# Attention's way back to channel layout: eight TensorE transposes against one VectorE transpose and a DMA round trip, with the conv branch placed first

## The reference

```python
h = rmsnorm(x, norm_mix_g[l])
proj = h @ w_in[l]
q, k, v, c_b, c_c, c_u, g_attn, g_conv = jnp.split(proj, split_idx, axis=-1)
...
attn = diff_attention(q1, q2, k1, k2, vh, rel_bias, lam)
attn = rmsnorm(attn, subln_g[l], SUBLN_EPS) * (1.0 - lambda_init)
y_attn = attn.reshape(B, T, ATTN_W) @ w_branch_attn[l]
y_conv = (c_b * causal_depthwise_conv(c_c * c_u, conv_w[l])) @ w_branch_conv[l]
merged = jax.nn.sigmoid(g_attn) * y_attn + jax.nn.sigmoid(g_conv) * y_conv
x = x + merged @ w_out[l]
```

## Time and profile before

| | |
|---|---|
| median of 3 runs | 1074.43 us (1073.64 to 1075.0) |
| profiled execution | 1073.29 us, span 1071.3 us |
| PE busy | 1063.6 us, 99% of the span |
| DVE, ACT, POOL busy | 746.9, 596.5, 185.1 us (70%, 56%, 17%) |
| granted TensorE clock | 0.999 of full speed |

### The profile page before, as it was taken

The page is one execution under the profiler, slowest core; times in us unless marked ns, Lnnn a source line. Parts: engine busy times, 40 slices in busy tenths (PEclk is TensorE's granted clock), DMA queues, the critical chain, the costliest instruction groups (busy, mean ns, idle before and its releaser), DMA issues.

```text
span 1071.3 us, 16564 instructions
## 1 busy us (share of the span) xinstructions
PE 1063.6 (99%) x5396; PEld 903.4 (84%) x5396; DVE 746.9 (70%) x948; ACT 596.5 (56%) x861; POOL 185.1 (17%) x337
## 2 busy tenths in 40 slices
PE   9999999999999999999999999999999999999997
PEld 7888888888889888888888888888888998888886
DVE  6766657868687866665776666668787888666654
ACT  7555445555785754444555444445657756555463
POOL 0354320000340022220002223000003300222300
PEclk9999999999999999999999999999999999999999
DMA  7888786655786688776668877566457957888872
GB/s 248 257 258 243 244 265 202 200 169 162 216 275 198 210 246 244 238 238 193 190 211 251 243 243 223 181 217 188 150 165 246 301 176 218 253 241 261 259 242 79
DMA packets 204551, 236.82 MB, mean 221 GB/s; under 512 B 17780, under 2 KB 179360, under 8 KB 204368
## 3 DMA queue, kind: packets, MB, share of 16 engines
q1 hardware_dynamic: 189968, 198.82, 59.6%
q0 software_dynamic: 14128, 36.76, 11.6%
q10 hardware_dynamic: 400, 0.51, 0.1%
HBM read 217.41 MB, written 18.62 MB: 220 GB/s over the span
## 4 chain that ended last, share of the span: by engine, by line
PE 98%; DVE 1%; DMA 0%; ACT 0%; issue 0%; DVEq 0%; ACTq 0%
PE acc L1636 21%; PE acc L1617 17%; PE acc L1618 17%; PE acc L1619 17%; PE acc L1645 11%; PE acc L1715 2%; PE acc L1714 2%; PE acc L1712 2%; PE acc L1640 1%; PE acc L1835 1%; PE mixed L1640 1%; PE score L1640 1%; PE acc L1836 1%; PE acc L1837 1%; PE score L1855 0%; DVE w_lo L1064 0%
## 5 line engine op out<-in xcount | busy, mean ns | idle before, releaser
L1064 DVE TENSOR_TENSOR w_lo<-raw,w_hi 128x1024 fp32r<-128x1024 f32 x382 | 455.6, 1205 | 226.5 <-ACT w_hi L657 225.7
L657 ACT CAST w_hi<-raw 128x1024 fp32r<-128x1024 f32 (+1 forms) x381 | 390.7, 1037 | 313.3 <-PE acc L1619 206.0
L1617 PE MATMUL acc<-w_hi,xm 128*128 128x512 f32 x816 | 319.6, 392 | 0.0
L1619 PE MATMUL acc<-w_lo,xm 128*128 128x512 f32 x816 | 318.0, 390 | 0.0
L1618 PE MATMUL acc<-w_hi,xm 128*128 128x512 f32 x816 | 317.9, 390 | 0.0
L1636 PE MATMUL acc<-hm,w_hi 128*128 128x512 f32 x656 | 206.3, 396 | 0.0
L1619 PEld LDWEIGHTS acc<-w_lo,xm 128*128 128x128 f32 x816 | 153.2, 188 | 31.8
L1617 PEld LDWEIGHTS acc<-w_hi,xm 128*128 128x128 f32 x816 | 153.3, 188 | 31.6
L1618 PEld LDWEIGHTS acc<-w_hi,xm 128*128 128x128 f32 x816 | 153.3, 188 | 31.2
L1645 PEld LDWEIGHTS acc<-hm,w_lo 128*128 128x128 f32 x720 | 133.4, 188 | 28.9
L532 POOL DMA_DIRECT2D hid_scratch<-sum x176 | 96.3, 554 | 346.5 <-DVE sum L1166 344.8
(11 more groups left out here) (191 smaller groups left out, 881.2 us busy)
## 6 DMA issues: line engine op xcount, KB each, us to landing
raw<-in_ffn_w_gate_dram SPq DMA_DIRECT2D x176, 256.0 KB, 3.1
raw<-in_ffn_w_up_dram SPq DMA_DIRECT2D x176, 256.0 KB, 3.6
raw<-in_ffn_w_down_dram SPq DMA_DIRECT2D x164, 256.0 KB, 3.5
raw<-in_w_in_dram SPq DMA_DIRECT2D x160, 256.0 KB, 3.3
hid_scratch<-sum POOLq DMA_DIRECT2D x176, 64.0 KB, 3.1
part<-hid_scratch POOLq DMA_DIRECT2D x44, 256.0 KB, 3.4
raw<-in_w_out_dram SPq DMA_DIRECT2D x32, 256.0 KB, 3.3
gate_scratch<-acc_lo POOLq DMA_DIRECT2D x64, 64.0 KB, 3.1
```

What stands on the lines that cost most here:

```text
L657: nc.scalar.copy(w_hi[:, s, 0:tiles, :], raw[:, s, 0:tiles, :]).then_inc(hi_split, 1)
L1064: nc.vector.tensor_tensor(w_lo[:, s, 0:tiles, :], raw[:, s, 0:tiles, :], w_hi[:, s, 0:tiles, :], ALU.subtract).then_inc(lo_split, 1)
L1617: nc.tensor.matmul(s[:, t, :], xh, wh[:, k], start=not u and not k, stop=False, skip_group_check=True)
L1619: mm = nc.tensor.matmul(s[:, t, :], xh, wl[:, k], start=False, stop=(u, k) == (GU_UNITS - 1, GK - 1), skip_group_check=True)
```

## The change

The eight PE transposes and the semaphore wait in front of them go. DVE turns the scaled attention in 32 x 32 blocks (into `v_tok`, which is free by then), POOL writes these to DRAM with four DMAs of 128 KB and reads them back with one of 512 KB (into `part`), and ACT applies the gain from there. POOL does this between the second and the third gate set. The order of the branches is exchanged: conv gates are projected as the first two sets, the conv branch is made ready first and multiplied first. Unrelated to this, in the first feed-forward block `join_squares()` moves ahead of one `lo()`.

```diff
-            gates[:, KT:KT + 4, :], gates[:, KT + 4:2 * KT, :], proj[:, 0:4, :], proj[:, 4:8, :])]
+            gates[:, 0:4, :], gates[:, 4:KT, :], proj[:, 0:4, :], proj[:, 4:8, :])]
+        attn_blocks_at = v_tok.rearrange("p t n -> p (t n)")
+        attn_back_at = part.rearrange("p k n -> p (k n)")
...
+        def gate_tile(n):
+
+            return (KT + 4 * n) % (2 * KT)
...
-                    by_token(w_in, l, GATE_COL + g * HALF)
+                    by_token(w_in, l, GATE_COL + gate_tile(g) * P)
...
-                    for w in (w_branch_attn, w_branch_conv):
+                    for w in (w_branch_conv, w_branch_attn):
...
-            def shuffle_gates():
+            def shuffle_attn(layer):
+
+                pool.wait_ge(attn_blocks, layer)
+                for a in range(QUARTERS):
+                    pool.dma_start(attn_dram.rearrange("(b i) (a f) -> a i b f", b=QUARTERS, a=QUARTERS)[a],
+                                   attn_blocks_at[a * QUARTER:(a + 1) * QUARTER, :].rearrange(
+                                       "i (b f) -> i b f", b=QUARTERS)).then_inc(attn_out, 16)
+                pool.wait_ge(attn_out, 16 * QUARTERS * layer)
+                pool.dma_start(attn_back_at, attn_dram).then_inc(attn_back, 16)
+
+            def shuffle_gates(layer):
 
                 for g in range(GATE_SETS):
+                    if g == 2:
+                        shuffle_attn(layer)
...
                 hi()
-                wait(act, (attn_turned, layers.now))
-                for b in range(2):
-                    last = nc.scalar.activation(
-                        attn[:, 2 * b:2 * b + 2].rearrange("p h t d -> p (h t d)"), side[b], ACT.Copy,
-                        scale=cur[:, P_SUBLN:P_SUBLN + 1])
-                last.then_inc(attn_gained, 1)
-                hi()
+                hi()
+                wait(act, (conv_ready, layers.now))
+                nc.scalar.copy(mix[:, N_HEADS:, 0:SEQ], conv).then_inc(conv_hi, 1)
+                hi()
+                wait(act, (attn_back, 16 * layers.now))
+                nc.scalar.activation(attn[:, :, :, :].rearrange("p h t (a n) -> p (h t) a n", a=QUARTERS),
+                                     attn_back_at.rearrange("p (a m n) -> p m a n", a=QUARTERS, m=N_HEADS * QT),
+                                     ACT.Copy, scale=cur[:, P_SUBLN:P_SUBLN + 1]).then_inc(attn_gained, 1)
                 wait(act, (attn_gained, layers.now))
                 nc.scalar.copy(mix[:, 0:N_HEADS, 0:SEQ],
                                attn[:, :, :, :].rearrange("p h t d -> p h (t d)")).then_inc(attn_hi, 1)
                 hi()
-                hi()
-                wait(act, (conv_ready, layers.now))
-                nc.scalar.copy(mix[:, N_HEADS:, 0:SEQ], conv).then_inc(conv_hi, 1)
                 have_table(ACT.Sigmoid)
                 gate_of_set()
...
                 for p in range(1, XPAIRS):
                     add_square(p)
+                join_squares()
                 lo()
-                join_squares()
                 lo()
...
                 taps(0)
                 lo()
+                wait(dve, (attn_scaled, layers.now))
+                nc.vector.transpose(attn_blocks_at.rearrange("p (b m n) -> p b m n", b=QUARTERS, m=N_HEADS * QT),
+                                    attn[:, :, :, :].rearrange("p h t (b n) -> p b (h t) n", b=QUARTERS)
+                                    ).then_inc(attn_blocks, 1)
                 taps(1)
...
-                wait(pe, (attn_scaled, layers.now))
-                for h in range(N_HEADS):
-                    for t in range(QT):
-                        col = ((h % 2) * QT + t) * P
-                        mm = nc.tensor.transpose(side[h // 2][:, col:col + P], attn[:, h, t, :], ident[:, :])
-                mm.then_inc(attn_turned, 1)
                 others_by_token()
...
-                            multiply(new_set(merge_sets[2 * n + j], len(merge_sets)), [mix[:, n * UK + k, :] for k in range(UK)], True, True,
+                            multiply(new_set(merge_sets[2 * n + j], len(merge_sets)), [mix[:, (1 - n) * UK + k, :] for k in range(UK)], True, True,
```

More of the change, by code:

```diff
@@ L225, in trunk @@
         gate_raw = [v.rearrange("p k n -> p (k n)") for v in (
-            gates[:, KT:KT + 4, :], gates[:, KT + 4:2 * KT, :], proj[:, 0:4, :], proj[:, 4:8, :])]
+            gates[:, 0:4, :], gates[:, 4:KT, :], proj[:, 0:4, :], proj[:, 4:8, :])]
+        attn_dram = nc.dram_tensor("attn_scratch", (P, N_HEADS * SEQ), F32, kind="Internal").ap()
         gate_dram = [nc.dram_tensor(f"gate_scratch{g}", (P, 2 * PAIR * SEQ), F32, kind="Internal").ap()
@@ L301, in trunk @@
         gate_by_token, gate_turned, gate_out = sem("gate_by_token"), sem("gate_turned"), sem("gate_out")
+        attn_blocks, attn_out, attn_back = sem("attn_blocks"), sem("attn_out"), sem("attn_back")
         gate_back = [sem(f"gate_back{g}") for g in range(GATE_SETS)]
@@ L610, in _ @@
             pool.wait_ge(bias_loaded, 32)
-            shuffle_gates()
+            shuffle_gates(1)
             shuffles()
             shuffles()
-            shuffle_gates()
+            shuffle_gates(2)
             pool.wait_ge(conv_ready, DEPTH)
@@ L1009, in _ @@
                         for j in range(2):
-                            t = n * 2 * PAIR + j * PAIR
+                            t = gate_tile(n) + j * PAIR
                             last = nc.scalar.activation(
@@ L1496, in _ @@
                 lo()
+                wait(dve, (conv_hi, layers.now))
+                nc.vector.tensor_tensor(mix[:, N_HEADS:, SEQ:2 * SEQ], conv, mix[:, N_HEADS:, 0:SEQ],
+                                        ALU.subtract).then_inc(mix_lo, 1)
+                lo()
                 wait(dve, (attn_hi, layers.now))
@@ L1501, in _ @@
                 lo()
[L1502 to L1505, removed]
                 turn_gates()
@@ L1515, in _ @@
                             n = 2 * g + j
-                            g_at = gates[:, bass.ds(i * (2 * PAIR) + (g * KT + j * PAIR), PAIR), :]
+                            g_at = gates[:, bass.ds(i * (2 * PAIR) + ((1 - g) * KT + j * PAIR), PAIR), :]
                             p_at = part[:, j * PAIR:(j + 1) * PAIR, :]
```

## The result

The changed kernel takes 1079.61 us (median of four runs, 1078.97 to 1083.93) against 1074.47 for the kernel before (1073.64 to 1075.0). The ratio is 1.0061 with an interval of 1.0049 to 1.0073: slower by 0.6%. The forecast was 1075.4, its range ended at 1079.0. The profiled execution took 1078.97 us with a span of 1077.1, that is 5.8 us more than the earlier trace rows were read from (1071.3).

A forecast was written before the change was run, and what follows sets the result against it. PE bounds the kernel and any lateness is paid in full. Waits of 2 x 1.5 less 1.74 and 0.23 gained give +1.0 us: 1074.3 against the profiled execution, 1075.4 on the timed runs' scale; range 1072.3 to 1079.0.

The forecast's parts named there:

- forecast 1.97: Gain on PE: eight transposes gone, 1.74 us over two layers, plus 0.23 us at the start from the moved `join_squares()`.
- T: Landing of the attention's read back from DRAM, first layer: forecast 312.4, bounds 310.3 and 313.5.
- b4: Branch-loop unit after b3: its `w_lo` ready at T + 8.5, wanted by PE at 319.4, 1.5 us late per layer.
- s: PE's wait at b4 in each layer, T - 310.9: 1.5 us at T = 312.4.
- b3: First attention unit of the branch loop: ready at T + 4.8, wanted at 316.5, late only from T = 311.7 on.
- b1: Branch-loop unit needing the conv product: DVE subtracts until 309.1, PE wants it at 310.8; expected to stay covered.
- I take 3.7: POOL's wait for the attention's four 128 KB writes to land, in us; 64 KB writes showed 3.10 to 4.07.
- 5.9: The attention's 512 KB read, issue to landing, in us; taken above the median of 5.6, range 4.4 to 6.6.
- the rival of the slow round trip: Attention's DMA round trip costs more than was won, from T = 313.0: +2.2 us, at the bound +3.2; chance 0.35.
- what is late next: Last merged tiles, wanted by the output projection's third unit near 341; last gates half a microsecond late, 1 to 2 us left.
- the third gate set's writes wait for the attention's read on POOL: POOL holds these writes from 303 to 307; their own read lands near 320.4, when ACT wants it at about 321.
- whose formula the prediction set aside: 2.0 us plus bytes at 436 GB/s per DMA: T near 308, nothing seen by PE; judged too low.

The follow-up runs named there:

- both edits and the sooner scaling: Changed kernel plus third gate set's writes before the attention's read on POOL, fourth gate set ahead of the attention, scaling one `hi()` sooner: 1078.23 us, ratio 1.0039.

## Why the prediction was wrong, and where it was right

**Right: the frame.** PE had no slack, lateness was paid in full, and the work taken off PE came out one for one as far as can be told: 0.9979 [0.997, 0.9988] without the DMAs is 2.3 us, with 1.3 to 3.2 possible, forecast 1.97.

**Right: the mechanism.** T to `w_lo` of b4 took 321.53 - 313.10 = 8.43 us (forecast 8.5), and s = T - 310.9 gives 2.2 for T = 313.10; b3 and b4 lost 1.35 + 0.84 = 2.19. In the second layer PE reaches b1 530.49 us later than in the first (841.28 against 310.79), so on the first layer's scale T is 844.53 - 530.49 = 314.04 and s = 3.1, as measured. As forecast, b4's deadline decides the total. Only the picture of the waits was wrong: the longer one stands at b3 and not at b4, since b3's wait has covered that much of b4's.

**Wrong in size: T.** "I take 3.7" for POOL's wait for the 128 KB writes and "5.9" for the read. The wait was 4.48 and 4.29, over the upper bound of 4.07; the read took 5.39 and 6.53, inside 4.4 to 6.6; the fourth write was issued by 303.23, not 302.8. The bounds were misread: "3.10 at the least and 4.07 at the most" holds for the rows picked in the earlier trace rows, not for the trace. Its waits for groups of 64 KB writes go from 2.87 us to 6.46, five of them over 4.07 (4.13, 4.75, 4.93, 4.95, 6.46). The longest, in the timeline of POOL before:

```profile
50.51 0.56 POOL L536 DMA_DIRECT2D part<-hid_scratch  x1 [6.46 <-DMA hid_scratch<-sum]
```

So the size of the writes is not shown to be what made the wait long: in the changed kernel the waits for the eight 64 KB writes of a gate set are 3.0 to 5.1 us, those for the four of 128 KB lie between. A wait of 4.5 us was a case to be counted on from the start. Against the forecast of 1.5 per layer, b3 and b4 cost 2.2 and 3.1: 2.3 us of the miss. This is the mechanism of the rival of the slow round trip, which had 0.35; its highest time without a halt was 1077.6, and what is missing to 1079.6 is mostly the next step.

**Wrong: "what is late next".** The prediction named the last merged tiles, wanted by the third unit of the output projection with 1 to 2 us left. It is the first unit that waits, because its PSUM bank is freed by DVE's take of b7 (`sum`, L1104). In the first layer DVE comes late to it by its own work: from the `lo()` at 320.35 to that take at 335.94 it idles for 0.26 us. It begins this stretch 5.3 us later than before (before: 315.06) and is still 4.1 us late 15.6 us on (before: 331.84). In the second layer the take waits for the last gates besides: ACT's sigmoid is held 1.46 us for the read back of the fourth set, as the ACT row at 866.64 shows, and DVE 0.47 us for ACT; PE's wait is 0.92. The prediction had these gates half a microsecond late on ACT and let it pass. Together 0.64 + 1.2 = 1.8 us, taken as 0. By this sum the time would have been 1077.8 without them, inside the range.

**Wrong: "the third gate set's writes wait for the attention's read on POOL"**, counted as costing nothing because their own read was wanted late. The reader asked for was the wrong one: whoever writes next into `acc_lo` waits too. In the changed kernel this hides behind the ACT chain: `acc_lo` is free at 317.6, ACT ends the gates at 318.98. It shows as soon as the wait for the attention is taken away (+0.17% instead of -0.11%), and DVE's wait for `acc_lo` is in three of the repairs.

**The sum again**, with the measured terms: 2.2 + 3.1 for b3 and b4, 1.8 for the output projection, -1.97 gained, and 0.46 because the second weight unit landed later in this execution (ACT rounds it at 8.75, before at 8.29): 5.6 of the 5.8 us between the spans. The first matmuls behind each of the four waits at b3 and b4 take 0.07 us longer (0.71 against 0.64 in PE's timeline), which is the rest within 0.1.

**By ratios**, the way from the kernel without the DMAs (-0.21%) to the changed one (+0.61%) goes over the traffic in a harmless order (+0.10%), POOL's order (+0.28%) and the wait for T (+0.44%). These are steps along one path and no independent costs: each wait hides part of another. Each of the four ratios has about 0.1% of uncertainty, and they come from two batches and the first measurement.

The Trainium skill, "DMA: Bandwidth & Descriptors", section "Anatomy of one DMA — SWDGE (gpsimd) path", whose formula the prediction set aside, would have put T near 308. The traces give 312.7 at the soonest and 317.0 at the latest in the first layer, and disagree with it in every kernel here. The advice of the Trainium skill, "VectorE: DVE Perf Modes", section "Rules for kernel authors", to use TensorE for such a transpose, came out right for this kernel: none of the DMA versions with the right result beat it.

## What to carry to other kernels

When a transfer is put into a queue, work out two things for everything behind it: when its reader needs it, and when the buffer it reads from is wanted again by its next writer. When an engine is held up, follow it until it has caught up, and not only to the first unit that waits for it: DVE, busy for 15.09 of 16 us from 320 to 336, made up 1.2 us of 5.3. A replacement with 12 us of latency for 0.87 us of the bound engine pays only if every instruction queued behind its wait has as much slack.

## What the hardware did that was not expected

**The granted TensorE clock.** In the kernel with the gates ahead of the attention's wait PE stood idle for 4.47 us before 322.27. The windows (busy us of PE, PEld, DVE, ACT, POOL; granted clock; DMA share; GB/s):

```profile
318.00:320.00 2.00, 0.00 (x0) 0.00 (x0) 0.20 (x1) 1.97 (x3) 0.00 (x0) 1.00 0.96 339
320.00:322.00 2.00, 0.00 (x0) 0.00 (x0) 2.00 (x3) 2.00 (x4) 1.75 (x4) 0.86 0.39 94
322.00:324.00 2.00, 1.73 (x8) 1.74 (x9) 1.88 (x3) 1.18 (x3) 2.00 (x4) 0.50 0.86 295
324.00:326.00 2.00, 2.00 (x11) 2.00 (x11) 1.88 (x3) 1.07 (x2) 1.14 (x3) 0.50 0.80 193
326.00:328.00 2.00, 2.00 (x12) 2.00 (x11) 1.45 (x3) 0.15 (x1) 0.00 (x0) 0.50 1.01 345
328.00:330.00 2.00, 2.00 (x17) 2.00 (x17) 1.97 (x3) 1.52 (x2) 0.56 (x1) 0.93 0.87 266
330.00:332.00 2.00, 2.00 (x19) 2.00 (x18) 1.37 (x3) 0.00 (x0) 0.00 (x0) 1.00 1.01 317
```

The clock falls from 2.4 to 1.2 GHz (0.50) and stays there for some 6 us; the matmuls in a window are 11 or 12 and not 19. A wait with such a fall costs more than its length. The length of the wait alone doesn't tell whether it happens. The kernel with only POOL's order changed has two waits of the same length at b3, one in each layer; the clock is 0.50 behind the first and 1.00 behind the second:

```profile
319.62 1.20 PE L1663 MATMUL acc<-hm,w_hi 128*128 128x256 f32 x4 [3.00 <-DVE w_lo L1083]
853.01 0.71 PE L1663 MATMUL acc<-hm,w_hi 128*128 128x256 f32 x4 [3.04 <-DVE w_lo L1083]
```

```profile
320.00:322.00 2.00, 2.00 (x11) 2.00 (x11) 1.16 (x2) 2.00 (x4) 0.15 (x1) 0.50 0.60 196
...
854.00:856.00 2.00, 2.00 (x18) 1.92 (x16) 1.77 (x3) 2.00 (x5) 0.76 (x2) 1.00 0.82 258
```

A wait of 2.13 us left the clock at 1.00 in the changed kernel (second layer), and one of 1.81 us was followed by 0.50 in the kernel with both edits and the sooner scaling (first layer). What decides is not shown by these runs. In the kernel with the read between the halves and the sooner scaling a wait of 2.02 us ended at 847.24, and the windows behind it read:

```profile
848.00:850.00 2.00, 2.00 (x12) 2.00 (x12) 1.88 (x3) 2.00 (x4) 2.00 (x4) 0.51 0.86 233
850.00:852.00 2.00, 2.00 (x13) 2.00 (x13) 1.88 (x3) 0.27 (x2) 0.12 (x1) 0.64 0.95 297
852.00:854.00 2.00, 2.00 (x19) 2.00 (x19) 1.97 (x4) 1.43 (x2) 0.00 (x0) 1.00 0.89 284
```

In PE's timeline three groups of six matmuls begin 1.28, 1.28 and 1.09 us before the next there (from 848.05 to 851.70), where 0.72 is the step at the full clock: 1.5 us are lost, on top of the wait of 2.02. The changed kernel's run of 1083.93 us had a mean clock of 0.994 against 0.998 in the profiled one; that this was the same fall was not profiled. The Trainium skill, "TensorE: Matmul & The Clock Gate", section "HAM oscillation — how this bites in real kernels", tells of a kernel in which PE falls to the lower clock in its wait for a DMA at every single step. The traces here agree in part: PE's waits are for DVE, which a DMA holds up, and behind some of them the clock is at 0.50, behind others at 1.00, as the rows above show.

**The wait for a group of writes from POOL** varies more than its size explains. The four writes of 128 KB are waited for 4.3 to 5.6 us behind the last issue in the runs with the changed kernel's order on POOL. The eight writes of 64 KB of a gate set are waited for 2.9 to 4.1 us in the kernel before, and up to 4.95 in the kernel before with only `join_squares()` moved, with the same DMAs in the same order.
